# Moving a head's output products one chunk later in a hybrid linear-recurrence layer on one Trainium2 core

## The chip, the core and the metric

The kernel runs on one core of one Trainium2 chip. The metric is the device time of one execution in microseconds (us). Three runs of the kernel before gave a median of 1894.4 us (1891.46 to 1896.7). TensorE (PE) does the matrix products and loads their weights (PEld), VectorE (DVE) and ScalarE (ACT) work elementwise, SyncE (SP) issues the transfers. Each engine takes its own instructions in their written order; semaphores order the engines among each other.

## The reference

One layer of an HGRN2 model over 256 latent tokens and 256 context tokens, D = 2048, 16 heads of 128, in float32:

```
a   = modulate(rms_norm(h))                        # context and latent
q, v, g = split(a @ w_in);  z_d = a @ w_f[d]       # d = forward, backward
log f = log_sigmoid(z) + log1p(lb exp(-z)),  k = (1 - lb) sigmoid(-z)
S_t = diag(f_t) S_{t-1} + k_t v_t^T,  o_t = S_t^T q_t   # both directions, context first
y   = (rms_norm_per_head(o_fwd + o_bwd) * silu(g)) @ w_o
h   = h + m2 * y;  h = h + m5 * swiglu(modulate(rms_norm(h)));  out = rms_norm(h)
```

The reference computes the recurrence in chunks of 64 tokens. The kernel computes it in blocks of 128 tokens: the scores of a block on seven levels of halving plus the diagonal, and the state that comes in from the context and from the other block.

## The kernel before

Weights stream from HBM as 496 chunks of 512 KB into four slots (`raw`). For each chunk ScalarE rounds a high part (`whi`, L440), VectorE subtracts the low part (`wlo`, L717), and TensorE makes three products for each pair of tiles (L1150 to L1152, L1165 to L1167). `whi` and `wlo` have three slots: ScalarE may write the copy for chunk c once chunk c-3 is used. TensorE waits for the low part ahead of every chunk.

`positions()` (L100) gives the order of the work in the scan stage. Eight pairs of heads have 16 chunks each: eight VQ chunks (value and query projections, 36 products of 256 columns) and eight Z chunks (the two gates, 24 products of 512 columns). Then come 32 G chunks (the output gate, 24 products of 256 columns), and then the WO chunks. Below, r is a chunk's place among its eight (0 to 7), and a position in the G chunks counts 0 to 31.

Beside these chunks run the heads, each as 13 tasks, j = 0 to 12, one in each chunk. A new head begins every eight chunks at r = 5, so that task j stands at r = (j + 5) mod 8, and tasks 8 to 12 of a head share chunks with tasks 0 to 4 of the next one, the older head first. In the G chunks the last two heads (14 and 15) are stretched: `tasks_tail` puts their task j at position s + (6j)//5 with s = 5 and 14. Each engine has a function `scan(j, n)` with its share of task j of head n. TensorE does its share in the middle of a chunk (`beside`); VectorE does it behind the low part of the next chunk, and ScalarE behind the high part of the next chunk, so both run up to a chunk ahead of TensorE as far as their waits allow.

The tasks by number, before:

- j = 0 to 2: VectorE cumulates the gates (L911 to L922) and builds the levels' exponents (L861, L862); ScalarE exponentiates them (j = 2, 3: L580, L583).
- j = 3, 4: VectorE multiplies the levels by keys and queries (L880, L881); at j = 4 ScalarE makes the state operands' exponentials (L566 to L577), for which the head before must have its outputs (`s_o`).
- j = 5: VectorE multiplies the state operands (L933 to L939).
- j = 6: TensorE transposes keys into `mx` and `ob` (L1284), for which the head before must be normalised (`s_on`), and makes the first block's scores (L1302, L1305). j = 7: ScalarE copies the turned keys, TensorE sums the states (L1291), VectorE places the first block's scores (`place(n, 0)`: the diagonal, L888, then seven masked copies, L892, each waiting for the one before).
- j = 8: TensorE makes the second block's scores; ScalarE and VectorE finish the states (L591, L955).
- j = 9: VectorE places the second block's scores (`place(n, 1)`); TensorE makes the 12 output products into `ob` (L1313 to L1316), for which both placings and the states must be done.
- j = 10: ScalarE squares the outputs (L595), TensorE sums the squares with one product (L1320). j = 11: ScalarE makes the reciprocal root (L600, L602). j = 12: VectorE normalises (L961).

Beside the tasks, VectorE adds up the modulation rows of `w_ada` (L813), clips and combines the gates (L826 to L845), and ScalarE does the gates' exponentials, the copies of v (L543) and of q, and in the G chunks at r = 2 the gate's Silu with two table loads (L611, L613). Before its Silu of q at r = 0 of a Z chunk ScalarE copies v from two banks, and for this waits for the outputs of the head three back. In chunks 34, 54, 82, 102, 131 and 150 of the scan stage TensorE also sums a part of the modulation (L1332). Behind the load of the first WO chunk SP waits for the last head's normalising and then fetches x, 2 MB, back from HBM (L396); the remaining WO loads are queued behind it.

Of the kernel before, what the change touches and what calls it, by code (L numbers as in the profile page):

```python
# [78 lines left out]
def head_slots():  # L79

    return [(-11, -4), (-3, -3), (5, -2), (13, -1), (21, 0), (29, 1)]


def tasks_at(p, groups=True):

    return [(p - s, off) for s, off in head_slots() if 0 <= p - s <= 12]


def tasks_tail(p):

    out = []
    for s, head, stretched in ((-11, HEADS - 4, False), (-3, HEADS - 3, False), (5, HEADS - 2, True), (14, HEADS - 1, True)):
        for j in range(13):
            at = s + (6 * j) // 5 if stretched else s + j
            if at == p:
                out.append((j, head))
    return out


def positions():  # L100


    for g in range(GROUPS):
        for p in range(BODY):
            kind = "Z" if p % 16 >= 8 else "VQ"
            tasks = [(j, 4 * g + off) for j, off in tasks_at(p) if 4 * g + off >= 0]
            yield C_B + g * BODY + p, kind, 2 * g + p // 16, p % 8, tasks
    for p in range(32):
        yield C_G + p, "G", p // 8, p % 8, tasks_tail(p)


def build(nc, x, c, ctx, c_ctx, w_ada, b_ada, norm_mix, norm_ffn, lb_logits, w_in, w_f, o_norm, w_o,
# [12 lines left out]
    with stack:  # L125
# [308 lines left out]
        def _(act):  # L434
# [122 lines left out]
            def scan(j, n):  # L557
                m = n % 2
                if j == 4:

                    act.wait_ge(s_cum, n + 1)
                    if n:
                        act.wait_ge(s_tr, 2 * n)
                        act.wait_ge(s_o, n)
                        act.wait_ge(s_s2, n)
                    act.activation(xs[:, 0, 0, :], pcum[:, 0, 0:P], ACT.Exp, bias=tot[:, m, 0, 0:1], scale=-1.0)  # L566
                    act.activation(xs[:, 0, 1, :], pcum[:, 0, P:2 * P], ACT.Exp, bias=pcum[:, 0, 2 * P - 1:2 * P], scale=-1.0)
                    act.activation(xs[:, 0, 2, :], pcum[:, 0, 2 * P:3 * P], ACT.Exp, bias=pcum[:, 0, 3 * P - 1:3 * P], scale=-1.0)
                    act.activation(xs[:, 1, 0, :], pcum[:, 1, 0:P], ACT.Exp)
                    act.activation(xs[:, 1, 1, :], pcum[:, 1, P:2 * P], ACT.Exp, bias=tot[:, m, 1, 0:1])  # L570
                    act.activation(xs[:, 1, 2, :], pcum[:, 1, 3 * P:TT], ACT.Exp)
                    act.activation(xi[:, 0, :], pcum[:, 0, T:TT], ACT.Exp)
                    for t in range(2):
                        act.activation(xi[:, 1, t * P:(t + 1) * P], pcum[:, 1, T + t * P:T + (t + 1) * P], ACT.Exp,
                                       bias=tot[:, m, 1, 2 + t:3 + t], scale=-1.0)
                    act.activation(etot[:, m, 0:1], pcum[:, 0, 3 * P - 1:3 * P], ACT.Exp)
                    act.activation(etot[:, m, 1:2], tot[:, m, 1, 3:4], ACT.Exp).then_inc(s_ex, 1)  # L577
                if j == 2:
                    act.wait_ge(s_sub, 2 * n + 1)
                    act.activation(eseq[:, :, 0:3 * T], eseq[:, :, 0:3 * T], ACT.Exp).then_inc(s_el, 1)  # L580
                if j == 3:
                    act.wait_ge(s_sub, 2 * n + 2)
                    act.activation(eseq[:, :, 3 * T:NL * T], eseq[:, :, 3 * T:NL * T], ACT.Exp).then_inc(s_el, 1)  # L583
                if j == 7:
                    for d in range(2):
                        act.wait_ge(s_tr, 2 * n + d + 1)
                        act.activation(kt[:, d, :, :], (mx, ob)[d][:, 0:384].rearrange("p (j t) -> p j t", j=3),
                                       ACT.Copy).then_inc(s_kt, 1)
                if j == 8:
                    act.wait_ge(s_st, n + 1)  # L590
                    act.activation(state[:, 0, :, :], mx[:, 0:256].rearrange("p (d v) -> p d v", d=2),  # L591
                                   ACT.Copy).then_inc(s_s1, 1)
                if j == 10:
                    act.wait_ge(s_o, n + 1)
                    act.activation(osq, ob[:, 0:T], ACT.Square).then_inc(s_osq, 1)  # L595
                if j == 11:
                    act.wait_ge(s_om, n + 1)
                    if n:
                        act.wait_ge(s_on, n)
                    act.activation(rstd[:, 0:T], mx[:, 0:T], ACT.Ln, bias=eps[:, :], scale=1.0 / P).then_inc(s_ol, 1)  # L600
                    act.wait_ge(s_ol, n + 1)
                    act.activation(rstd[:, 0:T], rstd[:, 0:T], ACT.Exp, scale=-0.5).then_inc(s_or, 1)  # L602
# [12 lines left out]
            for ck, kind, u, r, tasks in positions():  # L615
# [4 lines left out]
                p = (ck - C_B) % 16  # L620
# [43 lines left out]
            for u in range(2 * FG):  # L664
                for r in range(8):
# [3 lines left out]
                    if r == 2 and u % 2 == 1:  # L669
                        j = u // 2  # L670
# [43 lines left out]
        def _(dve):  # L714
# [180 lines left out]
            def scan(j, n):  # L895
# [55 lines left out]
                if j == 8:  # L951
# [4 lines left out]
                                                        scalar=etot[:, m, d:d + 1],  # L956
                                                        in1=mx[:, 256 + d * P:384 + d * P], op0=ALU.mult, op1=ALU.add)
                    last.then_inc(s_s2, 1)
                if j == 12:
                    dve.wait_ge(s_or, n + 1)  # L960
                    dve.scalar_tensor_tensor(out=oT[:, n, :], in0=ob[:, 0:T], scalar=vec[:, R_ONORM:R_ONORM + 1],  # L961
                                             in1=rstd[:, 0:T], op0=ALU.mult, op1=ALU.mult).then_inc(s_on, 1)
# [15 lines left out]
            for ck, kind, u, r, tasks in positions():  # L978
                if ck > C_B + KD // 2:
                    lo(ck + 1)  # L980
                p = (ck - C_B) % 16
# [134 lines left out]
        def _(pe):  # L1116
# [157 lines left out]
            def scan(j, n):  # L1274
                b, hh = (n // 2) % 2, n % 2
                KQ = keyq[b]
                V = vals[b][:, :, hh * P:(hh + 1) * P]
                if j == 6:
                    pe.wait_ge(s_xm, n + 1)
                    for d in range(2):  # L1280
                        if n:
                            pe.wait_ge(s_on, n)
                        for i in range(3):
                            last = pe.transpose((mx, ob)[d][:, i * P:(i + 1) * P], xs[:, d, i, :], ident[:, :])  # L1284
                        last.then_inc(s_tr, 1)
                if j == 7:
                    pe.wait_ge(s_kt, 2 * n + 2)
                    pe.wait_ge(s_vev, 2 * (n // 2) + 2)
                    for d in range(2):
                        for t in range(2):  # L1290
                            pe.matmul(mx[:, d * P:(d + 1) * P], kt[:, d, t, :], V[:, t, :], start=(t == 0), stop=(t == 1))  # L1291
                    for d in range(2):
                        last = pe.matmul(mx[:, 256 + d * P:384 + d * P], kt[:, d, 2, :], V[:, 2 + d, :], start=True, stop=True)
                    last.then_inc(s_st, 1)
                if j == 6 or j == 8:

                    t = (j - 6) // 2
                    pe.wait_ge(s_em, n + 1)
                    if n or t:
                        pe.wait_ge(s_pl, (2 * n + t) * NL)  # L1300
                    for li in range(NL):
                        last = pe.matmul(score[:, li // 4, (li % 4) * P:(li % 4 + 1) * P],  # L1302
                                         ebuf[:, 0, li, t * P:(t + 1) * P], ebuf[:, 1, li, t * P:(t + 1) * P],
                                         start=True, stop=True)
                    last = pe.matmul(score[:, 1, 3 * P:4 * P], ksum[:, t * P:(t + 1) * P],  # L1305
                                     KQ[:, hh, 1, T + t * P:T + (t + 1) * P], start=True, stop=True)
                    last.then_inc(s_sc, 1)
                if j == 9:
                    pe.wait_ge(s_pl, (2 * n + 2) * NL)
                    pe.wait_ge(s_s2, n + 1)  # L1310
                    for t in range(2):
                        o = ob[:, t * P:(t + 1) * P]
                        pe.matmul(o, V[:, 2 + t, :], pT[:, t, :], start=True, stop=False)  # L1313

                        pe.matmul(o, state[:, t, 0, :], xi[:, 0, t * P:(t + 1) * P], start=False, stop=False)
                        last = pe.matmul(o, state[:, 1 - t, 1, :], xi[:, 1, t * P:(t + 1) * P], start=False, stop=True)  # L1316
                    last.then_inc(s_o, 1)
                if j == 10:
                    pe.wait_ge(s_osq, n + 1)
                    pe.matmul(mx[:, 0:T], ones[:, :], osq, start=True, stop=True).then_inc(s_om, 1)  # L1320

# [37 lines left out]
            for u in range(2 * FG):  # L1359
                j = u // 2  # L1360
# [117 lines left out]
```

## Time and profile before

| | before |
|---|---|
| median of 3 runs | 1894.4 us (1891.46 to 1896.7) |
| profiled execution | 1894.17 us, span 1892.2 us, mean granted clock 0.992 |
| TensorE busy | 1839.9 us, 97% of the span |
| weight loads busy | 1689.6 us, 89% |
| VectorE busy | 1248.2 us, 66% |
| ScalarE busy | 877.4 us, 46% |
| transfers | 353.18 MB, 187 GB/s in the mean |

The scan stage with its heads lies between about 190 and 1000 us of the span. The rows below are read as follows. In a row of waits stand the engine, the instruction that waited, what it waited for, the sum of its idle time, how often, and the longest. In a row of the timeline stand the start, the duration, the engine, the line, the operation, out<-in and the shapes; in brackets the engine's idle time before it and what ended it. "PEq", "SPq" are sequencers. A matmul's end is modelled, and a matmul overlaps the one behind it.

### The profile page before, as it was taken

What the parts mean: (1) busy time and instruction counts of PE and PEld (TensorE: products, weight loads), DVE (VectorE), ACT (ScalarE), POOL (GpSimd) and SP (SyncE); (2) the same over time, 40 slices, a digit from 0 to 9 for tenths busy, and PEclk for the clock granted to TensorE, in tenths of its full rate; (3) what the DMA queues carried; (4) which work ended last, traced back from release to release, by engine and by line L of the source; (5) the groups of instructions that cost most, each with busy time, mean ns of one, the idle gap of its engine ahead of it and who ended that gap; (6) DMA issues with size and microseconds to landing.
All of it is one profiled execution on the core that took longest, in us unless ns stands there. A gap on an engine that the chain in (4) does not pass through costs nothing.

```text
span 1892.2 us, 31881 instructions
## 1 busy us (share of the span) xinstructions
PE 1839.9 (97%) x13319; PEld 1689.6 (89%) x13319; DVE 1248.2 (66%) x1935; ACT 877.4 (46%) x1202; POOL 0.2 (0%) x4
## 2 busy tenths in 40 slices
PE   7999999999999999998899999999999999999998
PEld 2278989898989898988899979999999999999996
DVE  6753878787979786979965465555555554544445
ACT  6762645353635344545544453333333333444444
POOL 0000000000000000000000000000000000000000
PEclk9999999999999989999999999999999999999999
DMA  9975545454445544444656547777677676555552
GB/s 369 365 263 158 176 139 159 149 156 133 146 134 158 158 141 123 150 132 152 220 179 214 180 123 218 220 224 217 209 220 226 215 215 211 187 179 183 185 183 96
DMA packets 175377, 353.18 MB, mean 187 GB/s; under 512 B 12737, under 2 KB 80642, under 8 KB 174594
## 3 DMA queue, kind: packets, MB, share of 16 engines
q1 hardware_dynamic: 175042, 351.11, 57.7%
q8 instruction: 104, 1.70, 0.4%
q14 instruction: 39, 0.32, 0.1%
q10 hardware_dynamic: 192, 0.05, 0.0%
HBM read 346.92 MB, written 4.19 MB: 186 GB/s over the span
## 4 chain that ended last, share of the span: by engine, by line
PE 81%; DVE 12%; issue 3%; ACT 2%; DMA 2%; SPq 0%; DVEq 0%; ACTq 0%
PE bank L1150 19%; PE bank L1151 19%; PE bank L1152 19%; DVE wlo L717 3%; PE bank L1165 2%; PE bank L1166 2%; PE bank L1167 2%; PE score L1302 2%; DVE work L892 2%; DVE aacc L813 2%; PE score L1150 2%; PE score L1152 2%; PE score L1151 2%; DMA arena<-in_x_dram 1%; PE ob L1152 1%
## 5 line engine op out<-in xcount | busy, mean ns | idle before, releaser
L717 DVE TENSOR_TENSOR wlo<-raw,whi 128x1024 fp32r<-128x1024 f32 x496 | 606.3, 1223 | 453.6 <-ACT whi L440 452.7
L1150 PE MATMUL bank<-ahi,whi 128*128 128x256 f32 (+1 forms) x2912 | 887.7, 305 | 7.7 <-DVE wlo L717 4.8
L1151 PE MATMUL bank<-alo,whi 128*128 128x256 f32 (+1 forms) x2912 | 881.3, 303 | 0.0
L1152 PE MATMUL bank<-ahi,wlo 128*128 128x256 f32 (+1 forms) x2912 | 881.2, 303 | 0.0
L440 ACT ACTIVATE whi<-raw 128x1024 fp32r<-128x1024 f32 x496 | 523.8, 1057 | 692.4 <-PE bank L1152 582.7
L1150 PEld LDWEIGHTS bank<-ahi,whi 128*128 128x128 f32 x2912 | 559.8, 192 | 28.0 <-DVE wlo L717 5.5
L1152 PEld LDWEIGHTS bank<-ahi,wlo 128*128 128x128 f32 x2912 | 559.4, 192 | 20.4
L1151 PEld LDWEIGHTS bank<-alo,whi 128*128 128x128 f32 x2912 | 559.9, 192 | 18.7
L813 DVE SCALAR_TENSOR_TENSOR aacc<-raw,cs,aacc 128x1024 f32<-128x1024 f32 x120 | 153.4, 1278 | 0.5
L1165 PE MATMUL bank<-whi,ahi 128*128 128x256 f32 x512 | 149.1, 291 | 0.0
L1166 PE MATMUL bank<-wlo,ahi 128*128 128x256 f32 x512 | 145.5, 284 | 0.0
L1167 PE MATMUL bank<-whi,alo 128*128 128x256 f32 x512 | 145.4, 284 | 0.0
L1165 PEld LDWEIGHTS bank<-whi,ahi 128*128 128x128 f32 x512 | 98.9, 193 | 1.3 <-issue 0.6
L1166 PEld LDWEIGHTS bank<-wlo,ahi 128*128 128x128 f32 x512 | 98.9, 193 | 0.4
L1167 PEld LDWEIGHTS bank<-whi,alo 128*128 128x128 f32 x512 | 98.7, 193 | 0.0
L892 DVE COPY_PREDICATED work<-masks,score 128x128 f32<-128x128 uint32 x224 | 67.7, 302 | 7.7
L1150 PE MATMUL score<-ahi,whi 128*128 128x256 f32 x240 | 68.0, 283 | 0.5 <-DVE wlo L717 0.5
L1152 PE MATMUL score<-ahi,wlo 128*128 128x256 f32 x240 | 67.9, 283 | 0.0
L1151 PE MATMUL score<-alo,whi 128*128 128x256 f32 x240 | 67.9, 283 | 0.0
L1302 PE MATMUL score<-work 128*128 128x128 f32 x448 | 55.2, 275 | 0.0
L682 ACT ACTIVATE ahi<-arena 128x256 fp32r<-128x256 f32 x44 | 18.4, 417 | 76.1 <-PE ob L1152 76.1
L1302 PEld LDWEIGHTS score<-work 128*128 128x128 f32 x448 | 53.1, 192 | 0.5
(217 smaller groups left out, 1774.5 us busy)
## 6 DMA issues: line engine op xcount, KB each, us to landing
raw<-in_w_ada_dram SPq DMA_DIRECT2D x168, 512.0 KB, 4.0
raw<-in_ffn_w_gate_dram SPq DMA_DIRECT2D x88, 512.0 KB, 4.2
raw<-in_ffn_w_up_dram SPq DMA_DIRECT2D x88, 512.0 KB, 4.2
raw<-in_ffn_w_down_dram SPq DMA_DIRECT2D x88, 512.0 KB, 3.5
raw<-in_hg_w_in_dram SPq DMA_DIRECT2D x128, 256.0 KB, 3.5
raw<-in_hg_w_f_dram SPq DMA_DIRECT2D x128, 256.0 KB, 3.5
raw<-in_hg_w_in_dram SPq DMA_DIRECT2D x32, 512.0 KB, 4.7
raw<-in_hg_w_o_dram SPq DMA_DIRECT2D x32, 512.0 KB, 3.5
```

Of the source, the lines that this page charges most:

```text
L440: act.activation(whi[:, ck % SPL, :], raw[:, q % RAW, :], ACT.Copy).then_inc(s_hi, 1)
L682: act.activation(yhi[:, k % 2, :], h1[:, k, :], ACT.Copy).then_inc(s_yh, 1)
L717: dve.tensor_tensor(wlo[:, ck % SPL, :], raw[:, SEQ["w", ck] % RAW, :], whi[:, ck % SPL, :].bitcast(F32), ALU.subtract).then_inc(s_lo, 1)
L813: dve.scalar_tensor_tensor(out=aacc[:, :], in0=block, scalar=cs[:, k, 0:1], in1=aacc[:, :], op0=ALU.mult, op1=ALU.add).then_inc(s_ac, 1)
L892: dve.copy_predicated(pT[:, t, :], masks[:, li * P:(li + 1) * P], src).then_inc(s_pl, 1)
L1150: pe.matmul(dst, w, ah, start=start, stop=False, skip_group_check=True)
L1151: pe.matmul(dst, w, al, start=False, stop=False, skip_group_check=True)
L1152: return pe.matmul(dst, wl, ah, start=False, stop=stop, skip_group_check=True)
L1165: pe.matmul(dst, ahi[:, k, tk], whi[:, s, o], start=st, stop=False, skip_group_check=True)
L1166: pe.matmul(dst, ahi[:, k, tk], wlo[:, s, o], start=False, stop=False, skip_group_check=True)
L1167: last = pe.matmul(dst, alo[:, k, tk], whi[:, s, o], start=False, stop=end, skip_group_check=True)
L1302: last = pe.matmul(score[:, li // 4, (li % 4) * P:(li % 4 + 1) * P], ebuf[:, 0, li, t * P:(t + 1) * P], ebuf[:, 1, li, t * P:(t + 1) * P], ...
```

## The change

Output products, squares, mean squares, reciprocal roots and the normalising product each come one task later: j = 10, 11, 12 and 13 in place of 9, 10, 11 and 12 (square and mean-square product share j = 11, as they shared 10). A head has 14 tasks in place of 13. `place(n, 1)` stays at j = 9. No wait, no buffer and no instruction is added or removed.

```diff
 def tasks_at(p, groups=True):
-    return [(p - s, off) for s, off in head_slots() if 0 <= p - s <= 12]
+    return [(p - s, off) for s, off in head_slots() if 0 <= p - s <= 13]
 def tasks_tail(p):
...
-        for j in range(13):
+        for j in range(14):
             at = s + (6 * j) // 5 if stretched else s + j
...
# ScalarE's scan
-                if j == 10:
+                if j == 11:
                     act.wait_ge(s_o, n + 1)
                     act.activation(osq, ob[:, 0:T], ACT.Square).then_inc(s_osq, 1)
-                if j == 11:
+                if j == 12:
                     act.wait_ge(s_om, n + 1)
...
# VectorE's scan
-                if j == 12:
+                if j == 13:
                     dve.wait_ge(s_or, n + 1)
...
# TensorE's scan
-                if j == 9:
+                if j == 10:
                     pe.wait_ge(s_pl, (2 * n + 2) * NL)
                     pe.wait_ge(s_s2, n + 1)
...
-                if j == 10:
+                if j == 11:
                     pe.wait_ge(s_osq, n + 1)
                     pe.matmul(mx[:, 0:T], ones[:, :], osq, start=True, stop=True).then_inc(s_om, 1)
```

By place among the eight chunks: output products from r = 6 to r = 7, square and mean-square product from r = 7 to r = 0, reciprocal root from r = 0 to r = 1, normalising from r = 1 to r = 2. In the G chunks head 13's output products go from position 6 to 7, head 14's from 15 to 17 (its mean-square product from 17 to 18), head 15's from 24 to 26 (mean-square product from 26 to 27, normalising from 28 to 29).

## Rows read from the trace of the kernel before

**Rows 1.** Waits by stretch: 240 to 860 us (two rows), then 860 to 1000.

```profile
PEld ob L1313 <- DVE work L892: 11.5, 11, 2.5
PE ob L1313 <- DVE work L892: 8.4, 6, 2.3
...
PEld ob L1313 <- DVE work L892: 9.6, 2, 5.3
```

**Rows 2.** Timeline: head 2's first output weights, then head 3's chunk with r = 6.

```profile
362.36 0.30 PEld L1313 LDWEIGHTS ob<-work,arena 128*128 128x128 f32 x2 [0.38 <-DVE work L892]
...
404.07 0.28 PE L1165 MATMUL bank<-whi,ahi 128*128 128x256 f32 x1
...
408.70 0.30 PEld L1313 LDWEIGHTS ob<-work,arena 128*128 128x128 f32 x2 [2.51 <-DVE work L892]
...
410.70 1.22 DVE L717 TENSOR_TENSOR wlo<-raw,whi 128x1024 fp32r<-128x1024 f32 x1
...
418.83 0.40 PE L1150 MATMUL bank<-ahi,whi 128*128 128x512 f32 x1
```

**Rows 3.** Timeline of head 9's chunk with r = 6; busy time and clock there.

```profile
691.93 0.28 PE L1165 MATMUL bank<-whi,ahi 128*128 128x256 f32 x1
...
696.56 0.30 PEld L1313 LDWEIGHTS ob<-work,arena 128*128 128x128 f32 x2 [2.51 <-DVE work L892]
...
711.39 0.40 PE L1150 MATMUL bank<-ahi,whi 128*128 128x512 f32 x1
...
692.00:706.00 14.00, 11.69 (x64) 11.49 (x64) 11.01 (x30) 2.82 (x3) 0.00 (x0) 0.68 0.24 76
```

**Rows 4.** Windows: length; PE, PEld, DVE, ACT, POOL busy (instructions); clock, DMA, GB/s.

```profile
359.00:409.00 50.00, 47.69 (x352) 44.85 (x351) 48.48 (x97) 26.84 (x44) 0.00 (x0) 1.00 0.55 169
409.00:457.00 48.00, 48.00 (x278) 42.20 (x277) 32.10 (x64) 20.05 (x31) 0.00 (x0) 1.00 0.39 121
843.00:953.00 110.00, 93.99 (x690) 90.09 (x688) 106.12 (x209) 62.92 (x100) 0.00 (x0) 0.94 0.58 184
```

**Rows 5.** Timeline: a Z chunk's second copy of v and middle; state operands and transposes.

```profile
417.59 0.60 ACT L543 ACTIVATE arena<-bank 128x512 f32<-128x512 f32 x1 [1.21 <-PE bank L1167]
...
421.58 0.39 PE L1150 MATMUL bank<-ahi,whi 128*128 128x512 f32 x1
...
386.18 0.76 DVE L939 TENSOR_TENSOR work<-work,arena 128x256 f32<-128x256 f32 x2
...
387.72 0.49 PE L1284 MATMUL mx<-ident,work 128*128 128x128 f32 x3
```

**Rows 6.** Timeline in the G chunks, positions 18 to 20.

```profile
947.14 0.47 ACT L600 ACTIVATE rstd<-mx,eps 128x256 f32<-128x256 f32 x1
...
947.97 0.39 ACT L566 ACTIVATE work<-work,tot 128x128 f32<-128x128 f32 x1
...
951.70 1.22 DVE L717 TENSOR_TENSOR wlo<-raw,whi 128x1024 fp32r<-128x1024 f32 x1 [0.92 <-ACT whi L440]
...
952.97 0.58 PE L1150 MATMUL bank<-ahi,whi 128*128 128x256 f32 x1 [2.07 <-DVE wlo L717]
```

**Rows 7.** A window behind that wait; timeline of head 15's mean-square product.

```profile
953.00:957.00 4.00, 4.00 (x21) 4.00 (x22) 4.00 (x9) 1.06 (x1) 0.00 (x0) 0.58 0.74 223
...
983.24 0.70 PE L1320 MATMUL mx<-rstd,ones 128*128 128x256 f32 x2 [0.99 <-ACT rstd L595]
```

**Rows 8.** Transfers ahead of the WO chunks, one's time to landing, a copy for it.

```profile
985.42 0.34 SPq L314 DMA_DIRECT2D raw<-in_hg_w_o_dram  x1
988.21 0.34 SPq L396 DMA_DIRECT2D work<-x_features  x1
988.90 2.12 SPq L314 DMA_DIRECT2D raw<-in_hg_w_o_dram  x2
...
raw<-in_hg_w_o_dram SPq DMA_DIRECT2D x1, 512.0 KB, 9.5
...
1000.77 1.06 ACT L440 ACTIVATE whi<-raw 128x1024 fp32r<-128x1024 f32 x1
```

## The prediction

> **What bounds the kernel now.** I read the page's first section, then the waits of TensorE by stretch, then the timeline around single waits, and last the busy time and granted clock by windows.
>
> By the table above TensorE is busy 97% of the span and VectorE 66%, so the change can only take from some 50 us in which TensorE is idle, and from time it spends at a low clock. In the scan stage the reader is to see one wait above all: the first output product (L1313) waits for the masked placing of the scores (L892). By the weight loads it cost 11.5 us in 11 waits up to 860 us, and 9.6 us in 2 waits after it [rows 1]. By the matmul rows the first number is 8.4 us in 6.
>
> Why it waits is seen at head 3 [rows 2]: its chunk (VQ, r=6) starts at 404.07, and L1313 loads its weights at 408.70, after 2.51 us of idling, so TensorE was at the middle by 406.2, half a VQ chunk being 2.1 us. In the 50 us up to there VectorE was busy 48.5 of 50; in the 48 us behind it only 32.1 of 48 [rows 4]. So VectorE falls behind from the Z chunk with r=6 to the next VQ chunk with r=6 and catches up in the Z chunks behind. TensorE needs the second block's scores in the very chunk in which VectorE places them, and this is where the lag shows.
>
> The stretch 843 to 953 us is another stage: VectorE is busy 106.1 of 110 us, TensorE 94.0 [rows 4]. There VectorE sets the pace, whatever the place where TensorE happens to wait for it.
>
> **The change part by part.** No instruction is added or removed: 16 times 12 output products, a Square, a mean-square product, Ln and Exp, and the normalising product come one chunk later (for the stretched heads 14 and 15 two positions for the output products).
>
> *Body, heads 0 to 12.* With the products at r=7, head 3 needs its scores in the middle of the next chunk. Without the stall the chunk with r=0 starts at 418.83 - 2.51 = 416.3 in the old times, or some 0.4 earlier, as the mean-square product has moved into it. Half a VQ chunk (2.1) and the 12 products (two weight loads take 0.30 us, so at most 1.8) lie ahead of it, so the products start at 412.0 or later; the scores are placed at 408.7. The low part for r=0 (L717 at 410.70, 1.22 long [rows 2]) is ready at 411.9, 4 us ahead. So nothing is late next here: the lag was less than one chunk, and VectorE catches up behind it as before. I take the whole 11.5 us, as every product has a weight load of its own ahead of it; the lower end is 8.4, the matmul rows' number, the upper 11.5 too.
>
> The Trainium skill (Perfetto Trace Analysis, section Identifying the Most-Contended Engine) calls matmul busy time a poor measure, because pipelined products look smaller in the trace, and has the weight loads read instead. By that page the term is 11.5, by the matmul rows 8.4, and the sum 3.1 us apart.
>
> *Clock in the body.* Heads 3 and 9 have the same work (both chunks also sum a modulation part) and the same wait, 2.51 us. From the chunk's first product to the second next chunk's it is 404.07 to 418.83, 14.76 us, at head 3 and 691.93 to 711.39, 19.46 us, at head 9; the granted clock is 1.00 around head 3 and 0.68 from 692 to 706 [rows 2 to 4]. The idle before head 9's products let the clock fall to its lower level, 1.2 GHz, and that cost 4.7 us. With the wait goes this drop: 4.7 us, lower end 0 if another wait brings such a drop.
>
> *Stage 843 to 953.* Waits for VectorE that go at one place come back at the next, as waits for L717; heads 13 and 14 gave 9.6 us there [rows 1], and I count 0 of it. The upper end is 9.6. What counts is when L717 of the chunk behind it is done, on which TensorE waits 2.07 us until 952.97; that L717 waited for ScalarE's copy, which started late because of the run L600, L602, then the eleven state exponents from 947.97 [rows 6]. Now a Square over the same 256 columns stands there, at most as long as the Ln (0.47), in place of Ln and Exp, which take the 0.83 us from 947.14 to 947.97: some 0.4 us gained.
>
> *New wait there.* Head 14's Square now stands at position 18 of the G chunks, behind a gate's two table loads; its mean-square product is in the same chunk, so TensorE will wait for it until about 947.5, with the products behind it queued. From there it has its own product, the rest of that chunk (half of 2.8) and one more chunk, some 4.7 us, to the place where it waits today until 952.97. So the wait costs nothing unless the clock falls. In 953 to 957 the clock was 0.58 after today's wait of 2.07, which cost 0.42 times 4, 1.7 us [rows 7]. That goes if TensorE is no longer idle just ahead, and is replaced by as much or more if the new waits (for L717 at position 17, some 4 us, and for the Square) pull it down: ends +1.7 and, with a drop as at head 9, -3.0. I take +0.8.
>
> *Head 15.* Its mean-square product waits 0.99 us behind the third gate's table loads [rows 7]; one chunk later it does not: 1.0 us gained.
>
> *SP's queue.* SP waits for head 15's normalising product before it fetches x back (L396), with the output weights queued behind. The transfers at 985.42 and 988.21 are released one G chunk apart, so the fetch comes 2.8 us later. The weight load issued at 988.90 took 9.5 us, to 998.4; 2.8 later is 1001.2, and ScalarE wants it at 1000.77 [rows 8]: 0.4 to 0.5 us lost; ends 0 and -2.8. I take -0.5.
>
> The Trainium skill (DMA: Bandwidth & Descriptors, section Queues, rings and completion order) says that descriptors of one row are taken in ring order but that completion is not first in, first out. By the second half the weight load might be done ahead of the fetch and the loss be 0; by the first it is the 0.5. The 9.5 us of a load of a quarter of the fetch's size, issued right behind it, speak for the first.
>
> *Covers that must hold.* The Square at r=0 of a Z chunk stands behind ScalarE's two copies of v, the second 417.59 to 418.19; with 0.5 for itself it ends before 418.8, and TensorE wants it at the middle, 421.58 [rows 5]: 3 us of cover. In VQ chunks Ln and Exp (0.8 us) now stand ahead of the state exponents, and the normalising product in the chunk that also multiplies them; at head 3 these end at 386.94 and TensorE transposes from 387.72 [rows 5]. TensorE comes there 0.4 us earlier, by the even head's own small wait [rows 2], so some 0.4 us of cover remain. VectorE's total work up to that point is the same.
>
> **Sum.** 11.5 + 4.7 + 0.4 + 0.8 + 1.0 - 0.5 = 17.9 us. The profiled execution took 1894.17 us (span 1892.2): 1876.3. It lies 0.2 us under the median of 1894.4, which changes nothing.
>
> **The rivals.**
> *The tail takes part of it back* (the clock falls in the new waits at positions 17 and 18, and the load behind the x fetch is late by the full 2.8): 0.8 becomes -3.0 and -0.5 becomes -2.8, gain 11.8, 1882.4. For it: 2.07 us of idle were enough at 951. Against: VectorE sets the pace there, so slow products have slack.
> *VectorE bounds the body too and the wait only moves* to L717 or to L892 a chunk later: a third of the 11.5 is kept, the drop at head 9 comes back, gain 4, 1890. For it: 48.5 of 50 us. Against: 32.1 of 48 behind it.
> *The other side: the transposes of the next head (L1284, r=3) become the wait.* TensorE, no longer held back, meets VectorE's state operands (L939) too early at the six odd heads, where cover is 0.4 us. A wait of 2.3 us with a drop of 4.7 each time is 42 us, 1918; it turns the sign from 3 us per odd head on. Against: VectorE's order up to there is as before, and TensorE is only 0.4 us earlier within each stretch, for VectorE waits for TensorE again in the Z chunks before it.
> *It does not do what it says*: the scores are late by a full chunk even so, the wait stays and moves by one chunk: 1893 to 1895. The lag of at most 2.5 us in the body speaks against it.
>
> **How the numbers follow.** Forecast case 0.72, tail 0.12, moved wait 0.06, transposes 0.06, no effect 0.04. Range: the high end is the sum with 8.4 for 11.5 and 0 for the clock and for all that follows: 1894.2 - 8.4 = 1886. The low end adds to 17.9 the 1.4 that the best ends of the tail's terms give (1.7 for 0.8, 0 for -0.5) and half of the 9.6, should VectorE not quite bound there: 1870. That leaves out the last three cases, 0.16. About 0.3% (5.7 us) is what a measurement of this kernel can tell from no change. Faster by more: 0.72, 0.12 and 0.05 of the moved wait; slower: the transposes' 0.06; within: 0.04 and 0.01 of the moved wait.
>
> **What would show it.** Waits on L1313 gone up to 860 us; no window at 0.5 of the clock around head 9; waits for L717 in 885 to 940 (old times) where those of heads 13 and 14 were; L1320 at position 18 waiting for L595, the one at position 27 not. It would be wrong if L1284 or L1313 showed waits at every odd head, or VectorE's idle time behind the VQ chunks (16 of 48 us) were gone with TensorE waiting for L717.

## The result: 15 us faster, 2.5 us over the forecast time

| | before | after |
|---|---|---|
| median | 1893.78 us (4 runs, 1891.46 to 1896.7) | 1878.79 us (4 runs, 1878.06 to 1879.82) |
| ratio | 1 | 0.992, 95% interval 0.9903 to 0.9938 |
| profiled execution, span | 1894.17, 1892.2 us | 1878.06, 1876.3 us |
| mean granted clock | 0.992 | 0.996 |
| TensorE busy | 1839.9 us (97%) | 1832.0 us (98%) |

The time lies in the range (1870 to 1886) and 2.5 us above the forecast of 1876.3. In the profiled executions the step is 16.1 us where the sum said 17.9.

The waits of TensorE after the change, 240 to 860 us and then 860 to 1000, as in [rows 1]:

```profile
PEld bank L1165 <- DVE wlo L717: 2.0, 2, 1.0
PEld mx L1284 <- DVE work L939: 1.9, 1, 1.9
PEld bank L1150 <- ACT arena L553: 1.1, 2, 0.6
...
PE bank L1165 <- DVE arena L826: 1.2, 2, 0.6
...
PEld bank L1150 <- DVE wlo L717: 10.0, 6, 3.9
PEld ob L1313 <- DVE work L892: 1.5, 1, 1.5
```

And the second row of before, 860 to 1000 us, which [rows 1] does not have:

```profile
PEld bank L1150 <- DVE wlo L717: 5.5, 3, 2.3
```

The eleven waits of L1313 up to 860 us are gone. Two small new kinds stand in the body, twice each: at the first VQ chunk of a pair (L1165; the weight loads name L717, the matmul rows L826) and at the first Z chunk (L1150 for L553). The wait of L1284, at 854.7 us, is one of before that now falls ahead of 860: it stands in the fourth G chunk. After 860 us L1313 fell from 9.6 to 1.5 us and L717 rose from 5.5 to 10.0. Over 840 to 1000 us all of TensorE's waits, by the matmul rows, are 16.9 us before and 17.1 after: there the waiting hasn't gone down.

Head 3's two chunks in the timeline after, beside [rows 2]:

```profile
402.83 0.28 PE L1165 MATMUL bank<-whi,ahi 128*128 128x256 f32 x1
...
404.69 2.31 DVE L892 COPY_PREDICATED work<-masks,score 128x128 f32<-128x128 uint32 x7
...
409.05 1.22 DVE L717 TENSOR_TENSOR wlo<-raw,whi 128x1024 fp32r<-128x1024 f32 x1
...
410.97 0.31 PEld L1313 LDWEIGHTS ob<-work,arena 128*128 128x128 f32 x2
...
414.58 0.40 PE L1150 MATMUL bank<-ahi,whi 128*128 128x512 f32 x1
```

The scores are placed by 407.0, the products load their weights at 410.97 without idle time before them. The low part for the next chunk is done at 410.27, 4.3 us before that chunk starts (forecast: 4). From the chunk's start to the second next chunk's it is now 11.75 us (before: 14.76), and the second next chunk, which now carries the mean-square product, is 0.46 longer (5.95 for 5.49).

Windows after: head 9's place [rows 3], head 3's two stretches and the stage that VectorE paces [rows 4], and the stretch behind the old wait of 2.07 us [rows 7], each moved by about what the chunks moved; columns as in [rows 4]:

```profile
686.00:700.00 14.00, 14.00 (x113) 13.66 (x112) 13.72 (x36) 7.31 (x8) 0.00 (x0) 1.00 0.36 111
355.00:405.00 50.00, 49.38 (x362) 46.65 (x361) 48.37 (x92) 26.72 (x44) 0.00 (x0) 1.00 0.51 159
405.00:453.00 48.00, 48.00 (x279) 42.24 (x278) 34.01 (x70) 19.81 (x31) 0.00 (x0) 1.00 0.42 132
828.00:938.00 110.00, 93.91 (x683) 89.17 (x683) 106.01 (x208) 60.75 (x98) 0.00 (x0) 0.95 0.57 182
939.00:943.00 4.00, 4.00 (x35) 3.95 (x34) 4.00 (x9) 1.91 (x2) 0.00 (x0) 1.00 0.75 239
```

No half clock around head 9. VectorE still has 14.0 idle of the 48 us behind the lag. The fourth row is the telling one: TensorE 93.9 and VectorE 106.0 of 110 us, the same as before (94.0 and 106.1). The products of heads 13 and 14 moved by one and two positions there, and that stage did not notice.

### The profile page after: what moved, and what is told of

Its sections match the earlier page's. It is cut to its first block, busy times and chain, and to the rows that moved or that the text cites. A ratio compares the mean times of both kernels' runs of the same rounds, so it can differ in the third digit from the quotient of the medians.

```text
span 1876.3 us, 31881 instructions
## 1 busy us (share of the span) xinstructions
PE 1832.0 (98%) x13319; PEld 1682.9 (90%) x13319; DVE 1248.2 (67%) x1935; ACT 875.4 (47%) x1202; POOL 0.2 (0%) x4
## 4 chain that ended last, share of the span: by engine, by line
PE 85%; DVE 8%; DMA 3%; ACT 2%; issue 2%; SPq 0%; ACTq 0%; DVEq 0%
PE bank L1150 19%; PE bank L1151 19%; PE bank L1152 19%; PE bank L1165 3%; PE bank L1166 3%; PE bank L1167 3%; PE score L1302 2%; DVE wlo L717 2%; PE score L1150 2%; PE score L1152 2%; PE score L1151 2%; DVE aacc L813 1%; DVE work L892 1%; DMA arena<-in_x_dram 1%; DVE work L862 1%
## 5 line engine op out<-in xcount | busy, mean ns | idle before, releaser
L1150 PE MATMUL bank<-ahi,whi 128*128 128x256 f32 (+1 forms) x2912 | 888.7, 305 | 13.6 <-DVE wlo L717 10.6
L717 DVE TENSOR_TENSOR wlo<-raw,whi 128x1024 fp32r<-128x1024 f32 x496 | 606.6, 1224 | 442.2 <-ACT whi L440 441.6
L1150 PEld LDWEIGHTS bank<-ahi,whi 128*128 128x128 f32 x2912 | 558.6, 192 | 35.6 <-DVE wlo L717 10.4
L813 DVE SCALAR_TENSOR_TENSOR aacc<-raw,cs,aacc 128x1024 f32<-128x1024 f32 x120 | 153.5, 1279 | 0.5
L1165 PE MATMUL bank<-whi,ahi 128*128 128x256 f32 x512 | 147.3, 288 | 1.3 <-DVE arena L826 1.2
L1165 PEld LDWEIGHTS bank<-whi,ahi 128*128 128x128 f32 x512 | 98.1, 192 | 2.7 <-DVE wlo L717 2.5
L1150 PE MATMUL score<-ahi,whi 128*128 128x256 f32 x240 | 68.0, 283 | 1.0 <-DVE wlo L717 1.0
```

Source lines behind the costliest of these rows:

```text
L717: dve.tensor_tensor(wlo[:, ck % SPL, :], raw[:, SEQ["w", ck] % RAW, :], whi[:, ck % SPL, :].bitcast(F32), ALU.subtract).then_inc(s_lo, 1)
L813: dve.scalar_tensor_tensor(out=aacc[:, :], in0=block, scalar=cs[:, k, 0:1], in1=aacc[:, :], op0=ALU.mult, op1=ALU.add).then_inc(s_ac, 1)
L1150: pe.matmul(dst, w, ah, start=start, stop=False, skip_group_check=True)
L1165: pe.matmul(dst, ahi[:, k, tk], whi[:, s, o], start=st, stop=False, skip_group_check=True)
```

## The experiments

All times are medians. The kernel before ran beside each group: 1895.14 us (23 runs, numbers 1 to 4), 1894.07 (21, numbers 5 to 8) and 1894.67 (11, numbers 9 to 11). A ratio is the time over that of the kernel before beside it, with its 95% interval; it is not the quotient of the two medians. "Tail" below means the stretch from the second G chunk (859 us before) to the second WO chunk, by the chunk starts of one trace: 143.9 us before, 142.0 after. In the first three and in numbers 8, 10 and 11 the tasks' order is chosen by head through a function `slot(j, n)` (j the task in the new numbering, n the head); `j - 1` for j >= 10 is the old place. The scan's code is otherwise that of the changed kernel.

**1. Heads 0 to 12 alone.**

```diff
+def slot(j, n):
+    return j - 1 if j >= 10 and n >= 13 else j
```

> Heads 0 to 12 as in the changed kernel, heads 13 to 15 (their products in the G chunks) as before. Theory: the gain is the wait of L1313 for the placing in the body and the clock drop at head 9, about 14 us of the change's 15 to 16; the stage with the G chunks gives only 1 to 2 us on balance. So 1879 to 1881, waits on L1313 up to 860 us gone, those of heads 13 and 14 (some 5 and 4 us) back. Rival: the G chunks carry a large part (their two waits were 9.6 us): then 1884 to 1889.

Measured: 1879.78 us (1878.74 to 1880.69), ratio 0.9922 (0.9909 to 0.9935). The body is nearly all of the gain.

**2. Heads 13 to 15 alone.**

```diff
+    return j - 1 if j >= 10 and n < 13 else j
```

> Heads 0 to 12 as before, heads 13 to 15 as in the changed kernel. Theory: VectorE sets the pace from 843 to 953 us, so the waits of heads 13 and 14 come back as waits for L717, and the gain is 1 to 2.5 us: 1891 to 1893 (head 15's 1.0 and a clock drop less, 0.5 lost by the later fetch of x). Rival: these waits were on the path, 9.6 us and their clock drops gone: 1880 to 1885.

Measured: 1893.97 us (11 runs, 1891.87 to 1896.61), ratio 0.9998 (0.999 to 1.0007). Less than expected, and not to be told from nothing. Its trace has a tail of 141.9 us, 2.0 shorter than before, but a body that is 3.0 longer, since the clock fell at head 3 too. TensorE's waits from 840 to 1000 us by the matmul rows, first with heads 0 to 12 alone changed, then with heads 13 to 15 alone:

```profile
PE ob L1313 <- DVE work L892: 9.3, 2, 5.1
PE bank L1150 <- DVE wlo L717: 4.9, 4, 3.0
```

```profile
PE bank L1150 <- DVE wlo L717: 11.3, 7, 3.8
PE mx L1320 <- ACT rstd L595: 2.7, 1, 2.7
...
PE ob L1313 <- DVE work L892: 1.2, 1, 1.2
```

The two rows of L1313 and L717 add up to 14.2 in the one and 12.5 in the other, and L1320 rose from 1.0 to 2.7. With L1284 all these waits are 18.0 us in the one and 17.5 in the other: the wait changed its name, as the prediction said when it counted 0 of the 9.6 us.

**3. The products stay, what follows them comes one chunk later.**

```diff
+    return 9 if j == 10 else j
```

> Output products stay where they were before (r = 6); square, mean-square product, reciprocal root and normalising come one chunk later as in the changed kernel. Theory: the products' wait is the cause, so waits on L1313 stay at 11 to 12 us up to 860 and the time stays at 1892 to 1894 (at most the 1.0 us of head 15's mean-square product is gained). Rival: the gain comes from taking the small steps out of crowded chunks of ScalarE and VectorE: then 1880 to 1886.

Measured: 1890.38 us (11 runs, 1885.68 to 1895.45; a twelfth took 9141.78 us and is left out), ratio 0.9978 (0.9965 to 0.9991): 4 to 5 us faster, which lies between the theory's 1892 to 1894 us and the rival's 1880 to 1886. Both missed. The waits of L1313 in the body are still there, 10.1 us in place of 11.1:

```profile
PEld ob L1313 <- DVE work L892: 10.1, 10, 2.1
```

Those at heads 3 and 9 are 2.1 us in place of 2.5, the others the same within 0.2. Two things can hold the gain. One is the tail, 141.6 us in this trace, as short as in the changed kernel: the wait of 2.07 us [rows 6] and head 15's of 0.99 [rows 7] are gone though the products stand where they stood, and L1320 of head 14 waits 2.8 in their place. So in the tail the small steps alone did what the whole change does there. The other is the clock: the two runs with the highest mean granted clock (0.996) took 1885.7 us, that with the lowest (0.989) 1895.5. How the gain is split between the two is not shown. The spread suggested that the price of a wait in the body is mostly a matter of what the clock does behind it, and led to numbers 8 and 11.

**4. The changed kernel once more.**

> The changed kernel again, beside the three parts on one chip. 1878 to 1880 by every theory; the parts of e1 and e2 should add up to it within 1 us if they do not act on each other.

Measured: 1879.0 us (1877.68 to 1880.46), ratio 0.9915 (0.9902 to 0.9928). Its body waits are the same to 0.1 us, with no half clock between 240 and 840 us. Its tail is 143.2 us, 1.2 longer than the first profile's, so tail terms of about 1 us read from one execution are within what executions differ by. The parts add up: 15.4 us in number 1 and 1.2 in number 2 make 16.5, against 16.1 here.

**5. and 6. VectorE relieved in the stage after 843 us.** The sixths of the modulation sums end earlier, so that 14 of the 16 of L813 (1.28 us each) that stood in the G chunks are done in the body; 5 on the kernel after, 6 on the kernel before.

```diff
-ADA_ENDS = (34, 54, 82, 102, 131, 150)
+ADA_ENDS = (34, 52, 71, 97, 114, 131)
...
-                if e < 5:
+                if e < 6:
                     pe.wait_ge(s_zc, 4 * (ADA_ENDS[e] // 16))
-                elif e == 5:
-                    pe.wait_ge(s_gev, 4)
```

> The changed kernel with the last 16 of VectorE's modulation sums (L813, about 1.28 us each, some 20 us) taken out of the stage after 843 us and done before it, by ending each sixth of the modulation earlier. Theory 'the tail is VectorE's': in the changed kernel TensorE still waits 10.6 us for L717, 2.8 for L1284, 1.5 for L1320 and 1.2 for L1313 between 840 and 1000 us, and all of these are late because VectorE is busy 119 of 142 us there; with 20 us less on it most of these waits go, 8 to 14 us, so 1865 to 1871 us, and the body (240 to 840) does not change by over 1.5 us. Rival 'the order sets the tail': the waits are chains of single steps that VectorE's load does not lengthen: 1877 to 1880. Rival 'VectorE's slack in the body is spent': new waits for L717 in the body eat the gain, 1872 to 1880 with TensorE's waits between 240 and 840 up by over 5 us.

> The kernel before with the same 16 modulation sums moved out of the stage after 843 us. Theory 'the tail is VectorE's': the tail's waits shrink as in the changed kernel (8 to 14 us), the ten waits of L1313 in the body stay at about 11 us and the clock's drops with them: 1881 to 1887, and the gain over the kernel before is within 3 us of what the same edit gains on the changed kernel. Rival 'the two edits take the same time': the waits of L1313 after 840 (9.2 us) are the change's to take and stay here, so the gain is under 5 us: 1890 or more.

Measured: 1874.8 us (1872.2 to 1876.71), ratio 0.9908 (0.9888 to 0.9927), and 1886.72 us (1883.55 to 1887.46), ratio 0.9962 (0.9948 to 0.9975). So, by the medians, 4 us on the changed kernel, where 8 to 14 were expected, and 7.4 us on the kernel before, just under that. Number 5's time lies in the range of its last rival, that VectorE's slack in the body is spent, but TensorE's waits there rose by 2 us, not by over 5. A part of number 6's gain is clock: its runs have 0.994 to 0.998, the kernel before beside it 0.989 to 0.995. The waits from 840 to 1000 us of the first:

```profile
PE bank L1150 <- DVE wlo L717: 4.8, 5, 1.6
PE mx L1320 <- ACT rstd L595: 3.8, 1, 3.8
PE mx L1284 <- DVE work L939: 2.9, 2, 1.7
```

L717 fell from 10.6 to 4.8, but L1320 rose from 1.5 to 3.8: a wait on a chain of single steps grew as that on VectorE's load shrank. By the chunk starts its tail (134.2 us) is 7.8 us shorter than in the first profile of the changed kernel, and its body up to 859 us 4.7 us longer. One sixth's sums on TensorE, 1.8 us, only moved from the one to the other. So the tail earned 6.0 us of some 18 that left VectorE, and the body lost 2.9, mostly to new waits at the first chunks of the pairs and of the G chunks. In number 6 the waits of L1313 in the body stay (12.7 us), as expected.

**7. The clipping of the gates ahead of the modulation sums.** At the boundary between two pairs, the sums (L813) of the last Z chunk come behind `clip_gates` on VectorE.

```diff
                 if p == 0 and C_B + 16 <= ck <= C_G:
                     clip_gates((ck - C_B) // 16 - 1)
+                    for i in ada_blocks(ck - 1):
+                        ada(i)
...
-                for i in ada_blocks(ck):
-                    ada(i)
+                if not (p == 15 and ck < C_G):
+                    for i in ada_blocks(ck):
+                        ada(i)
```

> The changed kernel with the modulation sums of one chunk (the last Z chunk of a group) put behind the clipping of the gates on VectorE instead of ahead of it. Theory: the new wait at the first VQ chunk of a group (L1165 for L826, 1.2 us in 2 times on TensorE, 2.0 on the weight loads) is a queue on VectorE, and goes: 1876.5 to 1878.5 us, no such wait in the trace. Rival: the clipping itself is late because of the head's steps of one chunk before, and the wait stays: 1878.5 to 1880.

Measured: 1878.67 us (1876.24 to 1879.71), ratio 0.9928 (0.9909 to 0.9947). Both theories get half: no wait for the clipping is left in the body, and by the chunk starts its body is 1.2 us shorter, but the time is that of the changed kernel (1878.8, 1879.0). From 840 to 1000 us (its line numbers are two lower):

```profile
PE bank L1150 <- DVE wlo L715: 12.4, 8, 3.8
```

It was 10.6 in 7 in the first profile of the changed kernel, and 11.9 in 8 in number 4, whose tail (143.2 us) is as long as this one's (143.3). So the tail may have taken the 1.2 us back, but that is not shown.

**8. Heads 3 and 9 alone, and 11. all heads but these two.**

```diff
+    return j - 1 if j >= 10 and n not in (3, 9) else j
...
+    return j - 1 if j >= 10 and n in (3, 9) else j
```

> Only heads 3 and 9 are changed, the other fourteen stay as before. Theory 'the two long waits carry the clock with them': the change takes two waits of 2.5 us (2.3 on TensorE) and, after each, the stretch at half clock that followed it in five of six such waits traced so far (1.6 to 4.7 us, mean of the six about 3.1): 4.6 + 6.2, less up to 1 for what comes late in their place: 9 to 11.5 us, 1883 to 1886 us, with the spread of its runs smaller than that of the kernel before (9 us). The eight shorter waits left (about 6 us on the weight loads, 3.8 on TensorE) then explain the rest, 4 to 6 us, to the changed kernel's 1879. Rival 'the clock falls somewhere in the body whatever the order': the two waits alone, 3.5 to 5 us: 1889.5 to 1891.5, with a window at half clock elsewhere between 240 and 840.

> The complement of the run with heads 3 and 9 alone: all heads but these two are changed. Theory 'the two long waits carry the clock, the eight short ones only their length': the eight waits of L1313 in the body go (6.1 us on the weight loads, 3.8 on TensorE), less the 2 to 3 us of new waits at the first chunks; the two of 2.5 us stay with what follows them at half clock: 4 to 6 us under the kernel before, 1888 to 1890 us, with runs as far apart as those of the kernel before (over 6 us). Rival 'half clock comes with the body as a whole': 1882 to 1886.

Measured: 1884.03 us (10 runs, 1883.08 to 1885.53), ratio 0.9958 (0.9944 to 0.9972), and 1885.08 us (6 runs, 1882.2 to 1891.03), ratio 0.9955 (0.994 to 0.9969). Number 8 came out as the theory said in its time: by the medians two heads of sixteen bring 10 us of 15, by the ratio 8.0 (5.3 to 10.6). Five of the 21 runs of the kernel before beside it had a clock of 0.994 or 0.995 and took only 1886.7 to 1889.1 us. The runs draw together from 12.5 us between the extremes (the kernel before beside them) to 2.5. In its trace nine shorter waits of L1313 are left from 240 to 840 us, and the clock is 1.00 behind all of them:

```profile
PEld ob L1313 <- DVE work L892: 6.5, 9, 1.7
```

Number 11 gained 9.6 us by the medians, 8.5 (5.9 to 11.4) by the ratio, where the theory said 4 to 6: its median lies in the rival's range, its spread (8.8 us) is the theory's. So the two gains make 16.5 (by the ratios) to 19.6 us (by the medians), more than the whole of 15 to 16, though by the ratios hardly. These are its weight loads of heads 3 and 9, and the 7 us some 2 us behind each:

```profile
407.13 0.30 PEld L1313 LDWEIGHTS ob<-work,arena 128*128 128x128 f32 x2 [2.12 <-DVE work L892]
...
695.81 0.30 PEld L1313 LDWEIGHTS ob<-work,arena 128*128 128x128 f32 x2 [2.11 <-DVE work L892]
```

```profile
409.00:416.00 7.00, 7.00 (x36) 7.00 (x37) 4.86 (x12) 1.81 (x3) 0.00 (x0) 0.55 0.24 75
698.00:705.00 7.00, 7.00 (x59) 6.95 (x60) 6.89 (x16) 3.39 (x4) 0.00 (x0) 1.00 0.40 124
```

With the other heads out of the way these two waits are 0.4 us shorter (2.1 as in number 3), and one of the two was followed by the lower clock, as one of two was in the profile of before. That number 11 took part of the clock's price too fits its mean clocks (0.991 to 0.996, median 0.994, for 0.992 beside it), but one trace can't show it. No other window between 240 and 840 us has a lower clock, which speaks against the rival's reason: what is left of the fall stands behind the wait that is left. The two of its runs with the highest mean clock (0.996) took 1882.3 us, 3.5 over the changed kernel, about the two waits.

**9. and 10. Both edits of the modulation on the changed kernel; and the edit of number 5 on number 1's order** (heads 13 to 15 as before). The diffs are those of 5 with 7, and of 5 with 1.

> The changed kernel with the two edits of the modulation together: the last 16 of VectorE's sums out of the stage after 843 us, and the sums of a group's last chunk behind the clipping of the gates. Theory: the wait at the first VQ chunks (1.9 us in 3 times on TensorE in the trace of the first edit alone) goes, and since TensorE's waits for L717 after 840 us are down to 4.8 us there, the tail no longer gives it all back: 1872 to 1874.5 us. Rival: the tail absorbs it, as it did when the second edit ran alone (1878.67 against 1878.8): 1874.5 to 1876.

> Heads 0 to 12 changed, heads 13 to 15 as before, and the last 16 modulation sums out of the stage after 843 us. Against the changed kernel with those sums out (1874.8) it tells what the change is worth on the last three heads once VectorE has less to do. Theory 'the gain of the last heads was eaten by VectorE': with 20 us less on VectorE the last heads' change is worth more than the 0 to 1.2 us it gave on its own, 3 to 5 us, so 1877.5 to 1880, with TensorE waiting 4 us or more for L892 at L1313 after 840 us. Rival 'it is worth nothing there': 1874 to 1876.

Measured: 1872.58 us (1870.96 to 1874.18), ratio 0.9889 (0.9875 to 0.9904), and 1878.09 us (1877.45 to 1878.38), ratio 0.9915 (0.9902 to 0.9928). Number 9 is the fastest version, 6 us under the changed kernel: with less on VectorE in the tail, the body's 1.2 us and a little more come through (2.2 us by the medians; its runs overlap those of number 5, which ran in another group). Number 10 is 3.3 us slower than number 5 by the medians, and their runs do not overlap, though they did not run side by side (the kernel before was 0.6 us apart). The traces say the same: the tail is 137.6 us in number 10, 134.2 in number 5 and 134.0 in number 9. So with VectorE relieved the change on heads 13 to 15 is worth some 3 us, where it was worth about 1 with VectorE full (1895.14 to 1893.97 in number 2, 1879.78 to 1879.0 in numbers 1 and 4; 0.8 to 2.0 us by the tails). Its waits from 840 to 1000 us:

```profile
PE bank L1150 <- DVE wlo L717: 5.2, 3, 3.4
PE ob L1313 <- DVE work L892: 4.5, 2, 3.2
```

The 4.5 us at L1313 are those that number 5 (0.4) has not, and there L717 (4.8) doesn't take them over; L1320, 3.8 for 1.0, takes a part.

## Why the prediction was right, and the step that was mis-sized

The starts of the chunks in the two traces, subtracted, give the gain so far at each place: 0.4 us at 280 us (old times), 14.0 at 859, 16.4 at the end of the G chunks, 15.9 from the output weights on.

**Body waits, 11.5: the step that was mis-sized, 8.9.** The body's 13.6 us less the clock's 4.7 (next point) leave 8.9. The mechanism is right: experiments 1, 8 and 11 take the waits by taking the heads. Two things lie between 11.5 and 8.9.

First, the new waits. They are on other lines than those that I priced (L1284 and L717 of the next chunk), at the r = 0 chunks:

```profile
370.06 2.47 DVE L826 TENSOR_SCALAR arena<-bank 128x512 f32<-128x512 f32 x4
...
370.88 0.36 PE L1165 MATMUL bank<-whi,ahi 128*128 128x256 f32 x1 [0.62 <-DVE arena L826]
...
603.06 1.92 ACT L583 ACTIVATE work<-work 128x2048 f32<-128x2048 f32 x1 [1.33 <-DVE work L862]
605.00 1.28 ACT L553 ACT_TABLE_LOAD   x1
...
606.94 0.19 PEld L1150 LDWEIGHTS bank<-ahi,whi 128*128 128x128 f32 x1 [0.56 <-ACT arena L553]
```

TensorE, no longer held back, comes to the next pair before VectorE has emptied the gates' banks (L826), and to the first Z chunk before ScalarE has emptied the queries' banks (L553, which stands behind an exponential that waits for VectorE). Each happens twice in the trace; by the chunk starts they cost about 0.7 and 0.4 us each, 2.3 us in all. I had asked what is late next only in the chunk of the products and at the transposes, not at each bank that TensorE refills. Experiment 7 took away the first kind and shortened the body by 1.2 us, though one small wait of the second kind came with it, so this part is shown; the second kind was not tried alone.

Second, the even heads' waits of 0.38 us before one weight load ([rows 2], 362.36; five of them). By the chunk starts heads 4 and 10 gained 0.30 and 0.32 us, where heads 0 and 6, without such a wait, gained 0.06: some two thirds of the length. At the odd heads whose clock stayed up the whole length by the weight loads was gained: head 3's two chunks and the next are 2.55 us shorter for a wait of 2.51, 2.3 by the matmul rows. The Trainium skill (Perfetto Trace Analysis, section Identifying the Most-Contended Engine) has the weight loads' busy share read in place of the matmuls'. Read so for waits, it agrees with this trace for the long ones, and overstates the short ones.

**Clock in the body, 4.7: right in the profile, by the run means somewhat more.** Head 9's chunk took 14.30 us before and takes 6.10 now: 8.2 us less: 4.3 more than head 3's 10.02 was the lower clock (and 0.4 in the next chunk), 2.5 the wait, 1.4 the products that moved on. But the profile of before is one draw, so that the 4.7 came out is in part luck. Whether the clock falls behind such a wait differs from one execution to the next, with the same wait at the same place. Each row is one trace:

| trace | wait by the weight loads | clock in the 7 us from some 2 us behind it |
|---|---|---|
| before, head 3 | 2.51 | 1.00 |
| before, head 9 | 2.51 | 0.50 |
| experiment 2, heads 3 and 9 | 2.53, 2.53 | 0.50, 0.56 |
| experiment 3, heads 3 and 9 | 2.10, 2.11 | 0.93, 0.50 |
| experiment 11, heads 3 and 9 | 2.12, 2.11 | 0.55, 1.00 |
| experiment 6, heads 3, 5 and 9 | 1.15, 3.11, 1.69 | 1.00, 0.90, 1.00 |

The rows of before, those of experiment 2, which leaves these heads as they were, and those of experiment 3:

```profile
411.00:418.00 7.00, 7.00 (x59) 6.95 (x60) 6.89 (x17) 3.37 (x4) 0.00 (x0) 1.00 0.42 129
699.00:706.00 7.00, 7.00 (x34) 7.00 (x34) 4.29 (x11) 1.75 (x2) 0.00 (x0) 0.50 0.23 75
```

```profile
412.00:419.00 7.00, 7.00 (x35) 7.00 (x34) 4.16 (x11) 1.75 (x2) 0.00 (x0) 0.50 0.23 75
704.00:711.00 7.00, 7.00 (x37) 7.00 (x37) 4.67 (x12) 1.78 (x3) 0.00 (x0) 0.56 0.23 75
```

```profile
411.00:418.00 7.00, 7.00 (x57) 7.00 (x57) 5.26 (x12) 2.79 (x3) 0.00 (x0) 0.93 0.23 75
700.00:707.00 7.00, 7.00 (x35) 7.00 (x34) 4.61 (x11) 1.48 (x1) 0.00 (x0) 0.50 0.23 75
```

In experiment 2 head 3 has the fall that before's profile did not have: its chunk takes 14.29 us, not 10.02. The mean clock of whole runs says the same. The kernel before, over the 55 runs beside the experiments:

| mean granted clock | runs | mean time, us |
|---|---|---|
| 0.989 and 0.990 | 8 | 1896.8 |
| 0.991 and 0.992 | 32 | 1895.0 |
| 0.993 | 9 | 1892.5 |
| 0.994 and 0.995 | 6 | 1888.0 |

The changed kernel's nine runs have 0.996 or 0.997. Against the 1888.0 of the runs with the highest clock it gains 9 us, near the 8.9 of the body's waits, though the tail's part is in it too; the other 6 of the 15 us in the medians would then be clock. So in the mean the clock in the body comes to about 6, where the sum had 4.7, and all the rest to about 9, where it had 13.2; the two errors partly cancel. That is a reading of run means, with the six runs picked by their clock, and not an experiment on the clock alone.

**Stage 843 to 953, +0.4; clock there, +0.8; head 15, +1.0.** Measured in the first pair of profiles: -0.4, +1.5 and +1.35, that is +2.4 for 2.2. These agree better than they deserve, and that is luck: in the second profile of the same kernel (number 4) that stage alone is 1.6 us longer. That the 9.6 us at L1313 give next to nothing is shown by experiments 2 and 3: heads 13 to 15 changed leave the time as it was, and the tail is as short with their products in the old place (141.6 us) as with them moved (142.0). Numbers 5 and 10 speak for VectorE as the reason. The waits are where they were foretold:

```profile
924.49 0.58 PE L1150 MATMUL bank<-ahi,whi 128*128 128x256 f32 x1 [3.68 <-DVE wlo L717]
...
934.54 0.70 PE L1320 MATMUL mx<-rstd,ones 128*128 128x256 f32 x2 [1.52 <-ACT rstd L595]
...
969.81 0.60 PE L1320 MATMUL mx<-rstd,ones 128*128 128x256 f32 x2
```

L717 at position 17 (3.68 for "some 4"), L1320 of head 14 behind ScalarE's Square, and head 15's L1320 without the 0.99 us of [rows 7]. The clock did fall at the new waits (0.50 from 924 to 930 us), as the rival of the tail had it, but falls of before went: the mean clock of the stage is 0.95, before 0.94 ([rows 4]), and the stage is 0.4 us longer. What the new fall cost by itself is not shown; that VectorE sets the pace there makes it likely to be little. The window behind the old wait (0.58 in [rows 7]) is at 1.00.

**SP's queue, -0.5: right in this pair, less in the others.** At the output weights the gain goes from 16.4 to 15.9. SP issues the fetch of x at 974.67, 2.9 us later against the chunks than in [rows 8] (974.67 + 16.4 - 988.21; forecast 2.8), and the load behind it is late:

```profile
984.85 1.06 ACT L440 ACTIVATE whi<-raw 128x1024 fp32r<-128x1024 f32 x1 [0.38 <-DMA raw<-in_hg_w_o_dram]
...
987.22 0.39 PE L1150 MATMUL score<-ahi,whi 128*128 128x256 f32 x1 [1.00 <-DVE wlo L717]
```

TensorE's wait there was 0.50 before. In all eight traces with head 15's later steps (experiments 2 to 5, 7, 9 and 11 and the changed kernel) the same load comes just too late, and that chunk is 0.06 to 0.49 us longer, 0.2 in the mean; in the other five traces it is as before. So the loss is shown; that it came out at the 0.5 is in part luck. The Trainium skill (DMA: Bandwidth & Descriptors, section Queues, rings and completion order) says that a row's descriptors are taken in ring order. By that rule the prediction had 0.5 rather than 0, and these traces lie between the two.

**The rivals.** The transposes (L1284) wait twice by the weight loads, as before, 3.2 us in place of 2.4, both behind 840 us, and at no odd head in the body. Behind head 3's lag VectorE kept 14.0 of its 16 idle us, so the wait did not move to it in the body. The rival of the tail was right in its mechanism (lower clock in the new waits) and wrong in its price.

Sum by the profiles: 8.9 + 4.7 - 0.4 + 1.5 + 1.35 - 0.5 = 15.55, with the 0.4 of the start the 15.9 that the spans differ by.

## What to carry to other kernels

Where a wait goes, walk on from it to every buffer that the freed engine refills until the lag is caught up, and look at who empties it: here two kinds of them took back 2 of 11 us. Price a wait with the clock that follows it, from several executions, and first remove the few longest: two heads of sixteen held half to two thirds of the gain. Where another engine is busy 106 of 110 us, take work off that engine first: here the same better order was then worth some 3 us, in place of about 1.

## What the runs showed of the hardware

The granted clock after an idle stretch of TensorE was not a matter of its length alone. After the eight waits of 2.1 to 2.5 us in the table it fell six times, five of them to the lower of its two levels for most of the 7 us (0.50 to 0.56), once for less (0.93). After the waits of up to 1.84 us in the bodies of all traces it never did. The same wait of 2.51 us, in the same work, left it at 1.00 at one head and brought it to 0.50 at another. What decides between the two is not shown here. A fall cost 1.6 to 4.7 us more than the wait itself, by the length of the chunks around it. Experiment 3, with 0.4 us off two such waits, is 4 to 5 us faster than the kernel before, but its shorter tail holds a part of that, and both its waits were followed by a fall.
